# Strassen block products in the down projection: 18 pairs of k tiles in alternating order, and weight sums by an accumulating DMA

## The reference, cut to what matters

```
def conv_ffn(h, w_up, conv_w, conv_b, w_down):
    u = h @ w_up
    up = jnp.pad(u, ((0, 0), (CONV_W - 1, 0), (0, 0)))
    uc = conv_b + sum(conv_w[i] * up[:, i:i + L] for i in range(CONV_W))
    a, val = jnp.split(uc, 2, axis=-1)
    return (jax.nn.silu(a) * val) @ w_down
...
    y = conv_ffn(h, w_up[l], conv_w[l], conv_b[l], w_down[l])
    h_res = h_res + rmsnorm(y, post_ffn_g[l])
return h_res[:, N_META:]
```

## Time and profile before

| | |
|---|---|
| Time, median of 3 runs | 1199.63 us (1199.42 to 1199.9) |
| Time of the profiled execution | 1199.66 us |
| Its span, first to last instruction | 1197.9 us |
| PE busy | 1186.6 us, 99% of the span |
| VectorE busy | 800.2 us, 67% |
| ScalarE busy | 653.7 us, 55% |
| GpSimd busy | 377.2 us, 31% |
| Bytes read from HBM | 209.53 MB, 177 GB/s with the writes |
| Loads of w_down | 88 of 512 KB |

### The profile page before, as it was taken

The page is one execution under the profiler, slowest core; times in us unless marked ns, Lnnn a source line. Parts: engine busy times, 40 slices in busy tenths (PEclk is TensorE's granted clock), DMA queues, the critical chain, the costliest instruction groups (busy, mean ns, idle before and its releaser), DMA issues.

```text
span 1197.9 us, 23215 instructions
## 1 busy us (share of the span) xinstructions
PE 1186.6 (99%) x8870; PEld 1131.3 (94%) x8870; DVE 800.2 (67%) x1140; ACT 653.7 (55%) x993; POOL 377.2 (31%) x183
## 2 busy tenths in 40 slices
PE   9999999999999999999999999999999999999997
PEld 8999999999999999999999999999999988888876
DVE  6865555464555346766666677666665699999998
ACT  7544545455784447545444444444454466666665
POOL 1233333333424442444444444444444310000000
PEclk9999999999999999999999999999999999999999
DMA  9655554554436664565565655556565556666562
GB/s 340 199 159 158 141 159 140 160 141 141 141 124 202 190 202 126 173 189 173 184 189 165 191 183 182 181 172 190 175 192 179 172 176 207 216 193 211 192 203 79
DMA packets 172906, 212.45 MB, mean 177 GB/s; under 512 B 6704, under 2 KB 158640, under 8 KB 172720
## 3 DMA queue, kind: packets, MB, share of 16 engines
q1 hardware_dynamic: 172416, 210.32, 57.2%
q10 hardware_dynamic: 432, 1.34, 0.3%
HBM read 209.53 MB, written 2.10 MB: 177 GB/s over the span
## 4 chain that ended last, share of the span: by engine, by line
PE 94%; DVE 4%; DMA 1%; ACT 0%; issue 0%; SPq 0%; DVEq 0%; ACTq 0%
PE psum L509 72%; PE psum L2090 10%; PE psum L2119 5%; DVE w_lo L573 2%; PE psum L1726 2%; PE psum L1957 1%; PE psum L1786 1%; DMA raw<-in_w_first 1%; PE psum L1812 0%; PE psum L2047 0%; PE psum L1890 0%; PE psum L1908 0%; DVE proj L1577 0%; PE psum L1813 0%; DVE proj L1685 0%; PE psum L1903 0%
## 5 line engine op out<-in xcount | busy, mean ns | idle before, releaser
L509 PE MATMUL psum<-a_hi,w_hi 128*128 128x258 f32 (+1 forms) x2360 | 673.8, 286 | 0.8 <-ACT temp L767 0.8
L509 PE MATMUL psum<-a_lo,w_hi 128*128 128x258 f32 (+1 forms) x2360 | 673.8, 286 | 0.0
L509 PE MATMUL psum<-a_hi,w_lo 128*128 128x258 f32 (+1 forms) x2360 | 670.0, 284 | 0.0
L493 POOL TENSOR_TENSOR w_lo<-raw,w_hi 128x1024 fp32r<-128x1024 f32 x144 | 361.5, 2510 | 576.6 <-ACT w_hi L489 576.6
L489 ACT ACTIVATE w_hi<-raw 128x1024 fp32r<-128x1024 f32 x307 | 322.4, 1058 | 328.1 <-PE psum L509 323.1
L509 PEld LDWEIGHTS psum<-a_hi,w_hi 128*128 128x128 f32 x2360 | 448.3, 190 | 6.1 <-issue 3.9
L509 PEld LDWEIGHTS psum<-a_lo,w_hi 128*128 128x128 f32 x2360 | 448.4, 190 | 0.0
L509 PEld LDWEIGHTS psum<-a_hi,w_lo 128*128 128x128 f32 x2360 | 446.0, 189 | 0.1
L493 DVE TENSOR_TENSOR w_lo<-raw,w_hi 128x1024 fp32r<-128x1024 f32 x164 | 216.2, 1320 | 249.4 <-ACT w_hi L489 247.3
L1518 DVE SCALAR_TENSOR_TENSOR proj<-proj,par 128x256 f32<-128x256 f32 x88 | 109.5, 1245 | 37.5 <-ACT proj L986 37.5
L567 ACT ACTIVATE w_hi<-raw 128x1024 fp32r<-128x1024 f32 x84 | 89.1, 1061 | 45.6 <-PE psum L2090 35.2
(11 more groups left out here) (264 smaller groups left out, 993.4 us busy)
## 6 DMA issues: line engine op xcount, KB each, us to landing
raw<-in_w_up SPq DMA_DIRECT2D x176, 512.0 KB, 3.6
raw<-in_w_in SPq DMA_DIRECT2D x88, 512.0 KB, 4.1
raw<-in_w_down SPq DMA_DIRECT2D x88, 512.0 KB, 4.3
raw<-in_w_out SPq DMA_DIRECT2D x32, 512.0 KB, 3.8
raw<-in_w_first SPq DMA_DIRECT2D x7, 512.0 KB, 10.9
xT<-in_features SPq DMA_DIRECT2D x3, 544.0 KB, 7.6
out<-proj SPq DMA_DIRECT2D x6, 256.0 KB, 2.4
temp<-in_post_ffn_g ACTq DMA_DIRECT2D x1, 1024.0 KB, 4.6
```

The source lines that it names most:

```text
L493: eng.tensor_tensor(w_lo[:, j % SPLIT, :], raw[:, j, :], w_hi[:, j % SPLIT, :], ALU.subtract)\
L509: mm = pe.matmul(psum[:, bank + m, 0:t1 - t0], w[:, j % SPLIT, cols], a[:, k, t0:t1], start=(k == 0 and step == 0), stop=(k == KT - 1 and ...
```

## The change

Each half now has 9 pairs `S` instead of 8. The first half is sss, four times Ss, one s, four times Ss, S, s; the second is ss, nine times Ss, ss. The signs of the block products are turned so that two of the four weight combinations are plain sums. For every pair `S` there is a third load: the right halves (512 columns) of both k tiles in one raw chunk, `sums`, and onto it GpSimd issues a DMA that reads the whole chunk of the first k tile (128 x 1024 words) from HBM and adds it in place. That makes two of the four combinations: unit 1 (1024 columns) is read from this chunk, so `w_diff` and its 1024-column subtraction are gone. VectorE keeps two additions of 512 columns. A plain pair's activations are split in one instruction of 512 columns on each engine instead of two of 256. The ninth pair's activation sums are four small VectorE instructions (`ninth_sum`).

```
-PASSES = ("sss" + "SsSss" * 3 + "SsS" + "s", "ss" + "SsSss" * 2 + "Ss" * 4 + "ss")
-SEVEN = ((0, 1, 2, 3, 4, 5, 6, 7), (4, 5, 6, 0, 1, 7, 2, 3))
+PASSES = ("sss" + "SsSsSsSss" + "Ss" * 4 + "S" + "s", "ss" + "Ss" * 9 + "ss")
+SEVEN = ((0, 1, 2, 3, 8, 4, 5, 6, 7), (4, 5, 6, 0, 1, 7, 2, 3, 8))
...
+        def loads(pr):
+
+            rows = [slice((2 * pr.pair + n) * P, (2 * pr.pair + n + 1) * P) for n in range(2)]
+            cols = slice(pr.half * CHUNK, (pr.half + 1) * CHUNK)
+            whole = [(pr.chunk + n, w_down[0, rows[n], cols]) for n in range(2)]
+            if not pr.seven:
+                return whole
+            right = w_down[0, 2 * pr.pair * P:2 * (pr.pair + 1) * P, cols.start + BANK:cols.stop]
+            return [(pr.sums, right.rearrange("(n p) c -> p n c", p=P))] + whole
+
+        def last_unit(c):
+
+            pr = max((o for o in DOWN if o.sums <= c), key=lambda o: o.unit)
+            if not pr.seven:
+                return pr.unit + c - pr.chunk
+            return pr.unit + (1, 2, 0)[c - pr.sums]
...
-            return (raw_of(pr.chunk + 1), w_diff[:, 0:CHUNK], raw_of(pr.chunk), w_diff[:, CHUNK:])[n]
+            return (raw_of(pr.chunk + 1), raw_of(pr.sums), raw_of(pr.chunk), w_last)[n]
...
             elif n == 0:
                 await_landed(eng, pr.chunk + 1)
+            elif n == 1:
+                eng.wait_ge(w_summed, 16 * (pr.seventh + 1))
             else:
-                eng.wait_ge(diffs_ready, 2 * pr.seventh + min(n, 2))
+                eng.wait_ge(diffs_ready, 2 * pr.seventh + n - 1)
...
+            for pr in DOWN:
+                if pr.seven:
+                    await_landed(pool, pr.sums)
+                    if pr.seventh > 0:
+                        pool.wait_ge(w_summed, 16 * pr.seventh)
+                    pool.dma_start(raw_of(pr.sums), w_down[0, 2 * pr.pair * P:(2 * pr.pair + 1) * P,
+                                                           pr.half * CHUNK:(pr.half + 1) * CHUNK], accum_op=ALU.add)\
+                        .then_inc(w_summed, 16)
...
+            def down_hi(pr):
+                act_e.wait_ge(act_made, 2 * pr.pair + 2)
+                if pr.plain >= 4:
+                    act_e.wait_ge(chunk_used, UP1 + plain_user(pr) + 2)
+                copy(d_pair(d_hi, pr), act_pair(pr)).then_inc(d_hi_ready, 1)
...
-                b1, b2 = raw_of(pr.chunk), raw_of(pr.chunk + 1)
+                b1, b2, both = raw_of(pr.chunk), raw_of(pr.chunk + 1), raw_of(pr.sums)
                 if part == 0:
                     for c in (pr.chunk, pr.chunk + 1):
                         await_landed(dve, c)
+                    dve.wait_ge(w_summed, 16 * (pr.seventh + 1))
+                    dve.tensor_tensor(b1[:, BANK:], b2[:, BANK:], both[:, 0:BANK], ALU.add).then_inc(diffs_ready, 1)
+                else:
                     if pr.seventh > 0:
                         dve.wait_ge(d_w_ready, max(o.unit for o in DOWN if o.seven and o.unit < pr.unit) + 4 - SPLIT)
-                    right = raw[:, pr.chunk % RAW:pr.chunk % RAW + 2, BANK:]
-                    dve.tensor_tensor(w_diff[:, 0:CHUNK].rearrange("p (n c) -> p n c", n=2), right,
-                                      b1.rearrange("p (n c) -> p n c", n=2), ALU.subtract).then_inc(diffs_ready, 1)
-                else:
                     dve.wait_ge(diffs_ready, 2 * pr.seventh + 1)
-                    dve.tensor_tensor(b1[:, BANK:], b2[:, BANK:], w_diff[:, 0:BANK], ALU.subtract).then_inc(diff_step, 1)
-                    dve.wait_ge(diff_step, pr.seventh + 1)
-                    dve.tensor_tensor(w_diff[:, CHUNK:], b2[:, 0:BANK], b1[:, BANK:], ALU.subtract)\
-                        .then_inc(diffs_ready, 1)
+                    dve.tensor_tensor(w_last, b2[:, 0:BANK], b1[:, BANK:], ALU.add).then_inc(diffs_ready, 1)
```

More of the change, by code:

```diff
@@ L143 @@
     chunk: int
+    sums: int
     plain: int
@@ L152, in down_pairs @@
 def down_pairs(n_pairs):
-    pairs, unit, plain, seventh = [], 0, 0, 0
+    pairs, unit, chunk, plain, seventh = [], 0, 0, 0, 0
     for half, kinds in enumerate(PASSES):
@@ L160, in down_pairs @@
             form, at = FORM_AT[half][n] if kind == "S" else (0, 0)
-            pairs.append(Pair(half, kind == "S", n, unit, 2 * len(pairs), plain, seventh, form, at, place))
+            ahead = 1 if kind == "S" else 0
+            pairs.append(Pair(half, kind == "S", n, unit, chunk + ahead, chunk, plain, seventh, form, at, place))
             unit += 4 if kind == "S" else 2
+            chunk += 2 + ahead
             plain += 0 if kind == "S" else 2
@@ L555, in product, with plain_user, d_pair, act_pair @@
             return banks(product_bank(half, n), product_bank(half, n) + 1)
+        def plain_user(pr):
+            return max(o.unit for o in DOWN if not o.seven and o.plain == pr.plain - 4)
+        def d_pair(rows, pr):
+            return rows[:, pr.plain % 4:pr.plain % 4 + 2, :].rearrange("p n t -> p (n t)")
+        def act_pair(pr):
+            return act[:, 2 * pr.pair * seq:(2 * pr.pair + 2) * seq]
+        def blocks_of(pr):
+            return pair_act[:, pr.pair] if pr.pair < N_SUMS else ninth_act
+        def sums_of(pr):
+            return pair_sums[:, pr.pair] if pr.pair < N_SUMS else ninth_sums
         def unit_hi(eng, pr, n):
@@ L1081, in _ @@
                         unit_hi(act_e, pr, n)
-                    if not pr.seven and pr.unit >= SPLIT:
-                        down_hi(pr, n)
+                    if not pr.seven and pr.unit >= SPLIT and n == 0:
+                        down_hi(pr)
                     if pr.form == 0 and pr.seven and n == 0:
@@ L1592, in prepare @@
                 dve.wait_ge(chunk_used, UP1 + after_sevens(half))
-                for n, (dst, a, b) in enumerate(((four, six, one), (three, seven, four), (four, five, four))):
+                for n, (dst, a, b, op) in enumerate(((four, one, six, ALU.subtract), (three, seven, four, ALU.add),
+                                                     (four, five, four, ALU.subtract))):
                     if n > 0:
                         dve.wait_ge(prep_step, 4 * half + n)
-                    dve.tensor_tensor(dst, a, b, ALU.add).then_inc(prep_step, 1)
+                    dve.tensor_tensor(dst, a, b, op).then_inc(prep_step, 1)
             def prepare_whole(half):
@@ L1601, in prepare_whole @@
                 dve.wait_ge(prep_step, 4 * half + 3)
-                dve.tensor_tensor(whole, product(half, 1), three, ALU.add).then_inc(prep_step, 1)
+                dve.tensor_tensor(whole, product(half, 1), three, ALU.subtract).then_inc(prep_step, 1)
             split_ahead_up(0, 4)
@@ L1647, in _ @@
                         dve.tensor_tensor(F_FIRST[t], src, F_FIRST[t], ALU.add).then_inc(f_added, 1)
-                between = p > 0 and DOWN[p - 1].seven and following and following.seven and not pr.seven
-                if between:
-                    differences(following, 0)
                 for n in range(4 if pr.seven else 2):
@@ L1655, in _ @@
                         unit_lo(dve, pr, n)
-                    if not pr.seven and pr.unit >= SPLIT:
-                        down_lo(pr, n)
-                    if following and following.seven and not pr.seven and not (between and n == 0):
+                    if not pr.seven and pr.unit >= SPLIT and n == 0:
+                        down_lo(pr)
+                    if following and following.seven and not pr.seven:
                         differences(following, n)
```

84 lines of the change are left out of this document (39 added, 45 removed).

## The result

The changed kernel is slower: 1223.11 us (median of 4, 1220.86 to 1224.63) against 1199.77, ratio 1.0193 (95% interval 1.0181 to 1.0206). The forecast was 1197.2, with a range of 1196.6 to 1208. The profiled execution took 1224.63 us with a span of 1222.9, so 25.0 us were added inside the span.

A forecast was written before the change was run, and what follows sets the result against it. Matmuls on PE were taken to set the time, with VectorE close behind in the down projection. 1199.66 - 1.36 - 1.12 + 0.2 = 1197.4, with the tail's 0.15 1197.2 us; range 1196.6 to 1208.

The forecast's parts named there:

- Fewer matmuls: In the down projection, two more pairs have 21 instead of 24 matmuls: 1.36 us off PE and the end.
- VectorE relieved: In the down projection, VectorE needs 9.3 us a couple against PE's 10.2, so 1.12 us of PE's waits go.
- The three gaps of the earlier trace: Places where a plain pair follows a seven-product pair and PE lost 0.26, 0.37 and 0.50 us.
- The first accumulating DMA: At the stage's first pair S, it may take 5 us from 964.85; cost 0 to 6 us, taken as 0.2.
- The later ones: At later pairs S, an accumulating DMA has about 10 us and fits if the DMA engines keep pace.
- Their pace: DMA engines in the stage: 308 GB/s, or 360 if an accumulating DMA costs two loads; no cost taken.
- rival A: Slower: accumulating DMA exceeds two loads' worth or takes over 10 us to land: 1205 at three loads' worth; chance 0.35.
- The price of a late sum: At the first pair S, each microsecond the DMA takes beyond 5 us was counted as a microsecond of PE.
- ScalarE's plain splits and the tail: New wait in `down_hi` costs nothing; in the tail three splits replace six, 3 x 0.05 us less on VectorE.

The follow-up runs named there:

- no_acc: Changed kernel with a tiny GpSimd memset raising the semaphore in place of the accumulating DMA, third load kept: 1197.76 us.
- scratch: Changed kernel with the accumulating DMA adding onto an unread buffer, its wait gone, the first started later, ninth pair's sums in their own buffer: 1197.78 us.
- experiment 2: Changed kernel with GpSimd memsets in series in place of the accumulating DMA: 1212.69 us with 15 memsets, 1198.13 us with 9.
- plain_copy: Changed kernel with GpSimd's DMA copying over the chunk instead of adding to it, waits kept: 1204.03 us.

## Why the prediction was wrong

- *Fewer matmuls, -1.36*: right. *VectorE relieved, -1.12*: about half of it came. `no_acc` and `scratch` lose 0.6 and 0.7 us in the stage where 1.2 were lost, and come out 2.1 and 2.0 us under the kernel before. The three gaps of the earlier trace rows are gone, but three of about 0.1 us appear in other places. VectorE's windows fell to 87.25, as the 9.3 us a couple asked (91 of 100 at most).
- *The first accumulating DMA, 0.2 us*: mis-sized. It could take 5 us and landed after 8.5; the estimate of 3.2 us, by which the term would be 0, was further off still. VectorE waited 4.28 us for it, and PE lost 2.5 us up to the 94th matmul (984.57 - 960.95 - 93 x 0.2267). It is a tenth of the loss.

```profile
964.70 1.01 POOL L798 DMA_DIRECT2D raw<-in_w_down  x1
...
973.29 0.69 DVE L1619 TENSOR_TENSOR raw<-raw 128x512 f32<-128x512 f32 x1 [4.28 <-DMA raw<-in_w_down]
```

- *The later ones, "about 10 us"*: this step failed. Both ends of the time were right. In `no_acc`, for the pair `S` of the last two rows in experiment 2, T (the start of the third `S` before it) is 1023.71: SyncE issues the right halves at 1034.3, T + 10.6 where I had T + 10, and VectorE's addition starts at 1048.56, T + 24.9 where I had T + 24.7. What failed are the two landings between them. The load of the right halves goes out right behind another one (two issues in this row, its own the second):

```profile
1033.97 0.81 SPq L712 DMA_DIRECT2D raw<-in_w_down  x2
```

  It lands 6.8 us after its issue here, not 4.5, and that leaves 7.3 us where I had 10.2. With the traffic of the accumulating DMAs such loads take longer still: by their issues and landings in the trace 8.1 us in the middle in the changed kernel, and 9.9 in the couple of `scratch` above. And I never gave the accumulating DMA a landing time of its own under that traffic; near 5 us was expected, 8.3 was measured. The 14.2 us from issue to use do not hold 8.1 and 8.3. "Both fit if the DMA engines keep pace": they do keep pace in `scratch`, and the wait still does not fit.
- *Their pace*: right, for what it was asked. The rows of `q0` say 1.8 copies' worth for an addition, and `scratch` carries it all at 0.96. That is near the two source reads that the prediction quotes from the Trainium skill, "Collectives: The Full Stack", section "The bandwidth ceiling: the fold count and why AG ≠ RS ≠ AR". The rival A was built on three loads' worth, which no run shows; its other clause, a DMA "over 10 us to land", was the true mechanism with the threshold too high: a median of 8.3 is enough. So the 0.35 for a slower ending, and its price of 1205, rested on the wrong quantity.
- *The price of a late sum.* I counted each microsecond of waiting as one microsecond of PE and no more. Of the 27.7 us lost 4.6 are steps at the low clock after the stops, which no term had.
- *ScalarE's plain splits and the tail*: nothing, as forecast; all the difference lies before the tail.

## What to carry to other kernels

When a value is to come by a load and then a second DMA onto it, add up the landings under the new traffic, one after the other, and set them against the time from the issue of the load to the first use of the value (14.2 us in the alternating stretches here, with or without the traffic). Bandwidth that suffices says nothing about that. Where a new wait stands in an in-order queue matters as much as its length: moved behind two splits that do not need it, it gave back three quarters of the loss. A work-around on a second engine has to be tried for what the two engines do to each other.

## What the runs showed of the hardware

- An accumulating DMA from HBM onto SBUF, 128 x 1024 words, costs the DMA engines 2.99 us, a copy of the same shape 1.67 (`plain_copy`); they land after 8.3 and 6.3 us. The issue holds GpSimd for 0.87 us.
- In `scratch` the DMA engines moved 291 GB/s over 100 us, 9 such additions among it, with loads of 512 KB landing after 6.6 us, and PE was not disturbed. A load issued 0.4 us behind another, in this traffic, took 9.9 us.
- In the changed kernel three stops of PE (2.77, 2.80 and 3.85 us from start to start) were followed by about 3 us at a granted clock of 0.5 (1.2 GHz), with matmuls 0.43 us apart; one of 3.44 and one of 2.32 us were not.
- A GpSimd addition of 1024 columns and VectorE's two-input instructions take turns: 2.4 us become up to 7.25, 1.22 become 2.45. Memsets on GpSimd over as long a time (the delay of 5.25 us) cost VectorE nothing.
